# Expert scores and queries of a two-layer network with product-key experts: one product of 512 columns for the high part of the weights, and a sum of two column halves

## The reference, cut to what matters

```python
q = (x @ w_query).reshape(T, 8, 2, 128)                 # 8 heads, two halves of a key
s = einsum('thpd,hpnd->thpn', q, sub_keys)              # 128 keys a half
s1, i1 = top_k(s[..., 0, :], 16); s2, i2 = top_k(s[..., 1, :], 16)
top_s, top_c = top_k(s1[..., :, None] + s2[..., None, :], 16)
idx = 128 * i1[top_c // 16] + i2[top_c % 16]            # one of 16384 experts
g = softmax(top_s)
act = gelu(einsum('td,thkd->thk', x, expert_down[idx]))
out = einsum('thk,thkd->td', g * act, expert_up[idx])
```

## Time and profile before

| | |
|---|---|
| median of the timed runs | 2203.69 us |
| profiled execution: its own time | 2204.31 us |
| profiled execution: span | 2202.4 us |
| TensorE busy with products | 2156.2 us (98%) |
| VectorE busy | 1375.7 us (62%) |
| ScalarE busy | 1235.8 us (56%) |
| GpSimd busy | 390.3 us (18%) |
| mean granted clock of TensorE | 0.992 |
| down products, layer 0 | about 197 to 598 us |
| down products, layer 1 | about 1140 to 1541 us |

### The profile page before, as it was taken

The page is one execution under the profiler, slowest core; times in us unless marked ns, Lnnn a source line. Parts: engine busy times, 40 slices in busy tenths (PEclk is TensorE's granted clock), DMA queues, the critical chain, the costliest instruction groups (busy, mean ns, idle before and its releaser), DMA issues.

```text
span 2202.4 us, 36208 instructions
## 1 busy us (share of the span) xinstructions
PE 2156.2 (98%) x14640; PEld 1970.6 (89%) x14640; DVE 1375.7 (62%) x2361; ACT 1235.8 (56%) x2086; POOL 390.3 (18%) x176
## 2 busy tenths in 40 slices
PE   8899999999999999997999999999999999999998
PEld 7789999999988888875899999999888888898897
DVE  7657867777755555547479567777555555423445
ACT  6654567777644444465545677776444444444463
POOL 1437810000000000022278200000000000243221
PEclk9999999999999999998999999999999999999999
DMA  6445555545466666652345555455566666754243
GB/s 217 144 135 163 183 172 163 163 164 172 161 196 194 196 192 192 193 166 86 115 157 187 166 171 165 162 164 172 189 194 192 193 197 191 254 182 144 87 135 115
DMA packets 104329, 373.41 MB, mean 170 GB/s; under 512 B 11564, under 2 KB 15044, under 8 KB 103780
## 3 DMA queue, kind: packets, MB, share of 16 engines
q1 hardware_dynamic: 104164, 371.11, 52.2%
HBM read 369.96 MB, written 1.10 MB: 168 GB/s over the span
## 4 chain that ended last, share of the span: by engine, by line
PE 92%; DVE 4%; ACT 2%; DMA 1%; issue 1%; POOL 0%; SPq 0%; ACTq 0%; DVEq 0%
PE ps L171 28%; PE ps L172 27%; PE ps L173 27%; PE ps L882 3%; PE ps L1862 1%; PE ps L1840 1%; DMA raw<-in_w_qk_dram 1%; DVE arena L1598 1%; DVE WL L159 1%; PE ps L267 1%; PE ps L861 1%; PE ps L1848 0%; PE ps L277 0%; PE ps L1322 0%; PE ps L1289 0%
## 5 line engine op out<-in xcount | busy, mean ns | idle before, releaser
L154 ACT ACTIVATE WH<-raw 128x1024 fp32r<-128x1024 f32 x680 | 717.5, 1057 | 540.6 <-PE ps L173 525.8
L171 PE MATMUL ps<-XH,WH 128*128 128x256 f32 x2816 | 806.6, 286 | 3.6 <-DVE XL L2146 2.8
L172 PE MATMUL ps<-XL,WH 128*128 128x256 f32 x2816 | 797.3, 283 | 0.0
L173 PE MATMUL ps<-XH,WL 128*128 128x256 f32 x2816 | 797.0, 283 | 0.0
L159 DVE TENSOR_TENSOR WL<-raw,WH 128x1024 fp32r<-128x1024 f32 x540 | 662.3, 1228 | 101.5 <-ACT WH L154 101.5
L164 POOL TENSOR_TENSOR WL<-raw,WH 128x1024 fp32r<-128x1024 f32 x140 | 349.6, 2501 | 1702.5 <-ACT WH L154 1701.5
L171 PEld LDWEIGHTS ps<-XH,WH 128*128 128x128 f32 x2816 | 540.3, 192 | 9.2 <-DVE XL L2146 3.0
L172 PEld LDWEIGHTS ps<-XL,WH 128*128 128x128 f32 x2816 | 541.0, 192 | 0.1
L173 PEld LDWEIGHTS ps<-XH,WL 128*128 128x128 f32 x2816 | 540.6, 192 | 0.0
L171 PE MATMUL ps<-WH,XH 128*128 128x512 f32 x960 | 380.2, 396 | 4.8 <-DVE XL L725 1.6
L172 PE MATMUL ps<-WL,XH 128*128 128x512 f32 x960 | 376.2, 392 | 0.0
(11 more groups left out here) (279 smaller groups left out, 1798.2 us busy)
## 6 DMA issues: line engine op xcount, KB each, us to landing
raw<-in_l_down_dram SPq DMA_DIRECT2D x256, 512.0 KB, 3.4
raw<-in_l_up_dram SPq DMA_DIRECT2D x256, 512.0 KB, 4.0
raw<-in_l_wq_dram SPq DMA_DIRECT2D x32, 512.0 KB, 3.4
raw<-in_w_qk_dram SPq DMA_DIRECT2D x24, 512.0 KB, 3.6
raw<-in_w_gates_dram SPq DMA_DIRECT2D x24, 512.0 KB, 3.5
raw<-in_l_nat_dram SPq DMA_DIRECT2D x16, 512.0 KB, 3.7
raw<-in_l_wout_dram SPq DMA_DIRECT2D x16, 512.0 KB, 3.8
raw<-in_l_win_dram SPq DMA_DIRECT2D x16, 512.0 KB, 4.1
```

What stands on the lines that cost most here:

```text
L154: a.activation(WH[:, i % NW, :], raw[:, i % NW, :], ACT.Copy).then_inc(w_high, 1)
L171: t.matmul(o, a[0], b[0], start=first, stop=False)
L172: t.matmul(o, a[0], b[1], start=False, stop=False)
L173: return t.matmul(o, a[1], b[0], start=False, stop=last)
```

## The change: what it does

`XH` and `XL` become the two halves of one array `X2`, so that for each step in depth the high and low columns lie side by side. A new function `two` takes the place of `three` in the queries and in the down blocks from 32 on: the high part of the weights meets all 512 columns in one product, and the low part meets the 256 high ones. Down blocks 0 to 31 keep `three`.

The result of such a block is then in two halves of a whole bank, which have to be added. For a pair of down blocks ScalarE copies the second halves of both banks to a new array `BESIDE` (`copy_beside`), VectorE adds them to the first halves (`down_add`: the tokens without gates out to SBUF, the others in place in PSUM), and only then ScalarE applies gelu (`gelus`). For the queries ScalarE copies the second halves to `QT` and VectorE adds (`queries`).

As a block takes a whole bank now, down blocks take turns in six banks, so that a pair's banks are written again six blocks later instead of eight, and the gate maps have one pair of banks: `products` of a group wait for the copy of the group in front. The steps move: the copy comes at the end of the step in which a pair ends, the addition and gelu in the next one, the product with the gates in the one behind that.

```diff
-        XH = sb("XH", [128, 8, 256], F32R)
-        XL = sb("XL", [128, 8, 256], F32R)
+        X2 = sb("X2", [128, 8, 2, 256], F32R)
+        XH, XL = X2[:, :, 0, :], X2[:, :, 1, :]
+        BESIDE = sb("BESIDE", [128, 2, 2, 256])
...
+        def two(t, bank, w, k, first, last):
+
+            t.matmul(PS[:, bank, :], w[0], X2[:, k, :, :].rearrange("p w t -> p (w t)"), start=first, stop=False)
+            return t.matmul(PS[:, bank, 0:256], w[1], X2[:, k, 0, :], start=False, stop=last)
...
         def open_tokens(c):
-            return 8 * sum(fold_chunk(s) <= c for s in range(GROUPS))
+            return 8 * sum(fold_chunk(s) <= c + 1 for s in range(GROUPS))
...
+        def down_bank(c):
+            return (c - WIDE + 4) % 6 if c >= WIDE else (c // 2) % 4
...
-            if s >= 2:
-                t.wait_ge(fold_a, 32 * l + s - 1)
+            if s >= 1:
+                t.wait_ge(fold_a, 32 * l + s)
...
-                if c % 2 == 0 and c >= 8:
-                    if open_tokens(c - 7):
-                        t.wait_ge(act_gated, N_HEAD * l + HEADS[c - 7])
+                if c == WIDE:
+                    t.wait_ge(it_up, l + 1)
+                elif c % 2 == 0 and c >= 8:
+                    before = c - (7 if c < WIDE + 4 else 5)
+                    if open_tokens(before):
+                        t.wait_ge(act_gated, N_HEAD * l + HEADS[before])
...
                 for k in range(8):
-                    m = three(t, o, [v[:, (down + c) % NW, k * 128:k * 128 + 128] for v in (WH, WL)],
-                              [v[:, k, :] for v in (XH, XL)], k == 0, k == 7)
+                    w = [v[:, (down + c) % NW, k * 128:k * 128 + 128] for v in (WH, WL)]
+                    if c >= WIDE:
+                        m = two(t, b, w, k, k == 0, k == 7)
...
+        def copy_beside(a, l, c):
+
+            n, b = pair_at(c), down_bank(c - 1)
+            a.wait_ge(w_used, bases(l)[1] + c + 1)
+            if c - 4 > WIDE:
+                a.wait_ge(added, N_ADD * l + ADDS[c - 4])
+            a.activation(BESIDE[:, n % 2], PS[:, b:b + 2, 256:512], ACT.Copy).then_inc(beside, 1)
+
+        def gelus(a, l, c):
+
+            k, g = open_tokens(c), G[:, c - 1:c + 1, :]
+            b, n = down_bank(c - 1), N_ADD * l + ADDS[c - 2]
+            if k < 256:
+                n += 1
+                a.wait_ge(added, n)
+                a.activation(g[:, :, k:256], g[:, :, k:256], ACT.Gelu_apprx_tanh).then_inc(act_tail, 1)
+            o = PS[:, b:b + 2, 0:k]
+            a.wait_ge(added, n + 1)
+            a.activation(o, o, ACT.Gelu_apprx_tanh).then_inc(act_head, 1)
...
                 high(a, down + c + 3)
+                if c > WIDE and c % 2 == 0:
+                    gelus(a, l, c - 1)
...
+        def queries(v, l, h):
+
+            q = QT[:, 2 * h:2 * h + 2, :]
+            v.wait_ge(wq_low, 8 * l + h + 1)
+            v.tensor_tensor(q, PS[:, 2 * (h % 2):2 * (h % 2) + 2, 0:256], q, ALU.add).then_inc(wq_up, 1)
...
+        def down_add(v, l, c):
+
+            k, n, b = open_tokens(c), pair_at(c), down_bank(c - 1)
+            v.wait_ge(beside, PAIRS * l + n + 1)
+            if k < 256:
+                v.tensor_tensor(G[:, c - 1:c + 1, k:256], PS[:, b:b + 2, k:256], BESIDE[:, n % 2, :, k:256],
+                                ALU.add).then_inc(added, 1)
+            o = PS[:, b:b + 2, 0:k]
+            v.tensor_tensor(o, o, BESIDE[:, n % 2, :, 0:k], ALU.add).then_inc(added, 1)
...
                 low_v(v, down + c + 2)
-                if c % 2 == 0 and c > 0:
-                    gate_vector(v, l, c - 1)
+                if c % 2 == 0 and c > WIDE:
+                    down_add(v, l, c - 1)
+                if c % 2 and c > WIDE + 1:
+                    gate_vector(v, l, c - 2)
```

More of the change, by code:

```diff
@@ L809, in build @@
         SPREAD, PACE, GROUPS = 29, 3, 32
+        WIDE = 32
+        beside, added = sem("down_beside"), sem("down_added")
         def fold_chunk(s):
@@ L828, in parts_g @@
                 return GH, GL_
-            return [v[:, 2 * (p % 3):2 * (p % 3) + 2, :].rearrange("p e t -> p (e t)") for v in (XH, XL)]
+            return [X2[:, 2 * (p % 3) + i, :, :].rearrange("p w t -> p (w t)") for i in range(2)]
         def bases(l):
@@ L889, in peer_tensor @@
             norm_tensor(t, n, XS)
-            def q_bank(pair, j):
-                if pair >= 2:
-                    t.wait_ge(wq_up, 16 * l + 2 * pair - 3 + j)
             for c in range(16):
                 pair, kh = divmod(c, 2)
-                chunk_T(t, wq + c, [PS[:, 2 * (pair % 2) + j, 0:256] for j in range(2)], 0, kh, 8,
-                        n if pair == 0 else None, lambda j: q_bank(pair, j))
+                wait_low(t, wq + c)
+                if kh == 0 and pair >= 2:
+                    t.wait_ge(wq_up, 8 * l + pair - 1)
+                for j in range(2):
+                    for kk in range(4):
+                        k = kh * 4 + kk
+                        if pair == 0 and j == 0:
+                            wait_x(t, n, k)
+                        m = two(t, 2 * (pair % 2) + j, [v[:, (wq + c) % NW, kk * 256 + j * 128:kk * 256 + j * 128 + 128]
+                                                        for v in (WH, WL)], k, k == 0, k == 7)
+                m.then_inc(w_used, 1)
                 if c >= 2 and c % 2 == 0:
@@ L902, in peer_tensor @@
                 if c < 8 and c % 2 == 0:
-                    t.wait_ge(wq_up, 16 * l + 13 + c // 2)
-                if c % 2 == 0 and c >= 8:
-                    if open_tokens(c - 7):
-                        t.wait_ge(act_gated, N_HEAD * l + HEADS[c - 7])
-                    else:
-                        t.wait_ge(act_tail, N_TAIL * l + TAILS[c - 7])
-                o = PS[:, (c // 2) % 4, (c % 2) * 256:(c % 2) * 256 + 256]
+                    t.wait_ge(wq_up, 8 * l + 7 + c // 4)
+                if c == WIDE:
[4 more added lines that the diff above has]
+                        t.wait_ge(act_gated, N_HEAD * l + HEADS[before])
+                    else:
+                        t.wait_ge(act_tail, N_TAIL * l + TAILS[before])
+                b = down_bank(c)
                 for k in range(8):
-                    m = three(t, o, [v[:, (down + c) % NW, k * 128:k * 128 + 128] for v in (WH, WL)],
-                              [v[:, k, :] for v in (XH, XL)], k == 0, k == 7)
+                    w = [v[:, (down + c) % NW, k * 128:k * 128 + 128] for v in (WH, WL)]
+                    if c >= WIDE:
+                        m = two(t, b, w, k, k == 0, k == 7)
+                    else:
+                        m = three(t, PS[:, b, (c % 2) * 256:(c % 2) * 256 + 256], w, [v[:, k, :] for v in (XH, XL)],
+                                  k == 0, k == 7)
                 m.then_inc(w_used, 1)
@@ L989, in peer_scalar @@
                     a.wait_ge(w_used, wq + c + 1)
-                    for j in range(2):
-                        a.activation(QT[:, 2 * pair + j, :], PS[:, 2 * (pair % 2) + j, 0:256], ACT.Copy).then_inc(wq_up, 1)
+                    a.activation(QT[:, 2 * pair:2 * pair + 2, :], PS[:, 2 * (pair % 2):2 * (pair % 2) + 2, 256:512],
+                                 ACT.Copy).then_inc(wq_low, 1)
             for c in range(128):
@@ L1007, in peer_scalar @@
                     split_g_scalar(a, l, 0)
-                if c % 2:
-                    ps, g, k = pair_view((c // 2) % 4), G[:, c - 1:c + 1, :], open_tokens(c)
+                if c % 2 and c < WIDE:
                     a.wait_ge(w_used, down + c + 1)
[L1011 to L1016, removed]
+                    a.activation(G[:, c - 1:c + 1, :], pair_view(down_bank(c)), ACT.Gelu_apprx_tanh).then_inc(act_tail, 1)
+                elif c % 2:
+                    copy_beside(a, l, c)
+            gelus(a, l, 127)
             for c in range(128):
@@ L1204, in peer_vector @@
                     split_g_vector(v, l, 0)
+            down_add(v, l, 127)
             gate_vector(v, l, 127)
```

41 lines of the change are left out of this document (24 added, 17 removed).

## The result

The changed kernel takes 2212.39 us (median of 5 runs, 2211.4 to 2212.75), against 2203.69 us before: 1.0041 times as long, 95% interval 1.0029 to 1.0053. It is slower, by 8.7 us, which is clear of the noise; 15 were forecast. (The prediction names two ranges, 2208 to 2233 in its sum and 2200 to 2236 beside its chances; the result lies in both.) The profiled execution has a span of 2210.9 us.

The account below looks back on a forecast made before the run. TensorE was taken to bound the kernel before; in the changed down products, VectorE and ScalarE waiting for each other. 2204.31 us plus 2 x (9.1 lost there - 1.7 gained in queries) gave 2219 us, range 2208 to 2233.

Parts of the forecast that it names:

- The mechanism: Down products: VectorE and ScalarE wait for each other, so TensorE waits before gate-map products; 9.1 us a layer slower.
- the ring: Down products: VectorE's additions, gelu, rows and L1147 wait in a circle; 19.77 us per two groups against TensorE's 18.58.
- The price of a step in depth: Queries and down blocks from 32: one product saved per step, 0.36 us becoming 0.347.
- The waits: TensorE before gate-map products: 0.2 and 1.1 us in turns, 18.8 us a layer over 14 two-group cycles.
- The lead of the two engines: From block 32 VectorE and ScalarE are ahead of TensorE, so TensorE first waits at group 3.
- the 0.5 us at the start of the up product: Behind the last down block: late addition and gelu of the last pair make TensorE wait 0.5 us.
- The additions: VectorE, per pair of down blocks: two additions over 512 elements together, 0.69 us pitch, bounds 0.55 and 0.9.
- What was called hidden: Query additions (5 us later picks under a 13.99 us wait), earlier reuse of banks, and loads: no cost.
- The queries' gain: Queries: 128 steps a layer each save one product, 1.7 us a layer gained in full.
- rival 3: Down products: VectorE is so late that TensorE also waits at the pair's banks; 2260 or 2233 us, chance 0.06.
- rival 1: Down products: load decides, VectorE keeps up and TensorE never waits; 2180.4 us, chance 0.12.
- Rival 4: Down products: waits pull TensorE's clock down, 3.35 us per half-clock stretch, 94 us in all; 2313 us, chance 0.03.

Follow-up runs that it names:

- e1: Changed kernel with a pair's two gelus moved behind the gate map's row instructions in ScalarE's step: 2187.16 us, 0.9926 of before.
- e4: Changed kernel with one extra ScalarE copy per group, in the step without row instructions: 2213.29 us, 1.0043 of before.
- e2: Changed kernel with gelus behind the row instructions and the copy of the gates one step later: 2183.14 us, 0.9911 of before.
- e5: Kernel before with only the queries changed to two products a step, down blocks keeping three: 2199.91 us, 0.9986 of before.
- e7: Kernel before with only the change's waits for banks added: 2203.35 us, 0.9999 of before.
- e6: Changed kernel with only the copy of the gates one step later, gelu left in place: 2216.45 us, 1.0063 of before.
- e3: Changed kernel with one extra ScalarE copy per group, in front of the second four row instructions: 2229.91 us, 1.012 of before.

## Why the prediction was right, and where its size was off

**The mechanism held.** Four forecasts of it can be read off the trace after: L897 is released by L1208; large and small waits take turns; VectorE idles before L1208 for ScalarE; ScalarE idles before gelu for the addition. e1 to e4 show that the ring is the cause: two moved instructions undo it, and an added one costs only where it stands on it. The price of a step in depth came as worked out. From the first product of group 0 to the first up product it took 304.75 us before (293.98 to 598.73) and 311.22 after (291.38 to 602.60). The saved products are 95 x 8 x 0.0133 = 10.1 us of that stretch, so 16.6 us were lost. Not all of it is waiting: e2's layer 1, where nothing waits, took 295.43 us, 9.3 less than before and not 10.1.

```profile
293.98 0.29 PE L882 MATMUL ps<-ONE 128*128 128x128 f16 x2
...
598.73 0.40 PE L171 MATMUL ps<-WH,GH 128*128 128x512 f32 x1
```
```profile
291.38 0.29 PE L897 MATMUL ps<-ONE 128*128 128x128 f16 x2
...
602.60 0.47 PE L172 MATMUL ps<-WH,GH 128*128 128x512 f32 x1
```

**The waits were over-sized.** The loss in this stretch is 16.6 us a layer where 19.3 were forecast, so the layer came out 6.5 us slower there and not 9.1. The ring in the middle was summed to 9.48 + 10.29 = 19.77 and took 9.35 + 10.29 = 19.64. At the end of the stage it took 20.22 (574.61 to 594.83) against 20.45:

```profile
574.61 0.69 DVE L1208 TENSOR_TENSOR ONE<-ONE,GP 128x1024 f16<-128x1024 f16 x1 [1.82 <-ACT ONE L981]
...
594.83 0.69 DVE L1208 TENSOR_TENSOR ONE<-ONE,GP 128x1024 f16<-128x1024 f16 x1 [1.85 <-ACT ONE L981]
```

From group 3 to 31 the L1208 lie 276.6 us apart, 19.76 a ring, where 19.92 were taken: 2.3 us for 14 rings.

In the middle, the half of the ring that was summed to 10.29 took 10.29. The error lies in the other half, 9.35 instead of 9.48, in ScalarE's part: 4.47 instead of 4.59. Three pitches (an instruction's start to the next one's) differ there. Four L981 in front of L991 took 1.18 us (461.00 to 462.18) and not 1.28. I had taken that from 410.56 and 411.84, but L958 waits for L1154, which ended at 411.09 + 0.72 = 411.81: the last 0.10 us were a wait that no bracket shows, since ScalarE's own last record hadn't ended. L991 took 0.35 (462.18 to 462.53) and not 0.47: the earlier trace rows are of group 12, where it copies 480 elements, and here 368 are left. Against that, the two gelus took 0.68 (460.32 to 461.00) and not 0.59, since L1011 also waits, for the second addition (L1225 ends at 460.66, L1011 starts at 460.69).

The lead of the two engines also lasted longer, which is worth only some 0.3 us. I had the first wait at group 3; in layer 0 it is at group 5:

```profile
338.75 1.02 PE L897 MATMUL ps<-ONE 128*128 128x128 f16 x15 [0.34 <-DVE ONE L1208]
```

The first wait was thus forecast two groups too early, and the 0.5 us at the start of the up product were 0.2 (602.29 to 602.60 against a pitch of 0.12).

**The additions** were sized well. The nearest rows were L1164 and L1057; the two of them took 0.333 and 0.331 us of pitch for 256 elements each, 0.66 us against the 0.69 taken.

```profile
L1225 DVE TENSOR_TENSOR ps<-ps,BESIDE 128x512 f32<-128x512 f32 x4 | 2.8, 695 | 1.4 <-ACT BESIDE L999 1.4
```

An addition that reads and writes PSUM takes 695 ns for 512 elements, as L1057 did.

**What was called hidden was hidden.** The picks came 13.99 us before they were asked for, as in the earlier trace rows, in spite of eight additions:

```profile
280.12 0.42 DVE L1176 CAST IB<-ps 128x256 bf16<-128x256 f32 x1 [13.99 <-PE ps L885]
```

The queries' gain is smaller than forecast, though. From the first query product to the first product of group 0 it took 148.92 us before (145.06 to 293.98) and 147.60 after (143.78 to 291.38), in both layers: 1.3 us gained a layer where the prediction has 1.7 "in full". That term was too large by 0.4 us a layer, and e5 shows the same without the changed down products. The banks (rival 3) are excluded for the order before by e7, and in the trace after every wait of TensorE in the down products is for L1208.

**The rest of the difference.** Twice 6.5 us in the down products, less twice 1.3 in the queries, is 10.3 us; the span grew by 8.5. The other 1.8 us lie in stages that the change doesn't alter, and such stages vary between executions: the first query product of layer 0 starts at 142.24 us in the profile of e6 and at 145.06 in that of e4, which have the same instructions up to there. From the 14.8 us of the forecast to the 8.5 of the span it is thus 5.3 less for the waits, 0.8 more for the queries, and 1.8 less by what varies, which no forecast could know.

**The rivals.** Load (rival 1) was the strongest against me: its 2180 us are what e2 reaches, 2183.14, with the same load in another order. So its claim that both engines have room was right, and its claim that room is enough was wrong. Rival 4 fell too: 14 idle times a layer of up to 1.27 us, one in every second group, didn't lower the clock, which is 1.00 over the stage; nor did e3's, of up to 1.59 us. The Trainium skill ("TensorE: Matmul & The Clock Gate", A second HAM failure mode: psum-queue depth-cycling) tells of a kernel in which short idles between groups of products made the clock swing; these idle times did not. The price that the prediction gives for a half-clock stretch, 3.35 us, was too high by its own rows: of the 6.7 us TensorE worked for 5.20, so half of that, 2.6 us, is what the clock cost. Only rival 4's 94 us hang on it.

**What stays open.** In e2 groups of layer 0 take 9.31 and 9.47 us in turns, those of layer 1 9.31 us always. Nothing waited there, and the products themselves were slower by some nanoseconds each; over the layer that makes 2.3 us (297.77 against 295.43), about what e2 lies above my 2180.4. The changed kernel's first groups in layer 0 take turns in the same way, and e1's don't. No run told its cause apart.

## What to carry to other kernels

Before work is moved onto engines with idle time, follow the waits: if the added work stands between two waits that already tie two engines to each other, its pitch is added to a ring, and the ring is compared with the bound engine's time, not the engines' busy shares. Sum the ring from the starts in the timeline, since idle time inside it is no room. When a ring turns out to be the bound, move the instruction that waits behind those that others wait for: here that turned a change that lost 0.4% into one that gains 0.9% (e2). Try such moves one by one: of the two, the late copy alone (e6) made the kernel slower. And look at the distance from the releaser's end to the start of what it releases, not only at idle times on record: a constant short distance is the mark of a wait, even where no idle time is shown.

## What the runs showed of the hardware

TensorE's L897, when it waited for VectorE's L1208, started 0.26 us behind the recorded end of L1208 (456.16 to 456.42, 465.51 to 465.77), and 0.25 or 0.26 us behind it in 21 groups of layer 0. Between ScalarE and VectorE the same distance was 0.03 us (L981 to L1208, 454.13 + 1.31 to 455.47).

A TensorE product that goes on after the gate map's products has a longer first distance, 0.31 us for 512 columns (466.66 to 466.97) instead of the usual 0.23:

```profile
466.66 0.47 PE L178 MATMUL ps<-X,WH 128*128 128x512 f32 x1
466.97 0.28 PE L179 MATMUL ps<-X,WL 128*128 128x256 f32 x1
```
